# Key selection in a two-block kernel: the third query tile's rounds beside the first and second tile's, instead of behind them

## The reference

```
# i_q (512, 8 heads, 64), i_k (512, 64) layer-normed, i_w (512, 8)
rel   = relu(einsum('bqhd,bsd->bqhs', iq_b, ik))      # per block of 128 queries
score = einsum('bqh,bqhs->bqs', iw_b, rel)
score = where(key <= query, score, -inf)
_, idx = top_k(score, 128)                            # min(256, 512 // 4) = 128
```

## Time and profile before

| | us |
|---|---|
| median of three runs | 2519.91 |
| the profiled execution | 2520.09 |
| span of its trace | 2518.3 |
| TensorE busy | 2481.8 |
| VectorE busy | 1619.7 |
| ScalarE busy | 1205.7 |

### The profile page before, as it was taken

One profiled execution on the slowest core, in us unless ns is written; L12 is line 12 of the kernel. 1 busy time (PEld: TensorE's weight loads), 2 busy tenths in 40 slices (PEclk: granted clock), 3 DMA queues, 4 the chain that ended last, 5 costly groups with the idle time before them and its releaser, 6 DMA issues.

```text
span 2518.3 us, 37877 instructions
## 1 busy us (share of the span) xinstructions
PE 2481.8 (99%) x15440; PEld 2070.1 (82%) x15440; DVE 1619.7 (64%) x2585; ACT 1205.7 (48%) x2030; POOL 75.2 (3%) x114
## 2 busy tenths in 40 slices
PE   9999999999999999999999999999999999999998
PEld 7999888888877777878999888777776788888887
DVE  6888348866764554357887257766877655677733
ACT  6556244666555455245555246544333454444421
POOL 0111000000000000000110000000000000000000
PEclk9999999999999999999999999999999999999999
DMA  5776332222222222333775323211111112333232
GB/s 173 175 179 154 108 100 92 77 76 75 84 68 68 76 66 77 91 92 101 176 177 151 98 93 101 76 41 37 44 43 52 59 55 88 94 99 101 88 100 72
DMA packets 80525, 237.82 MB, mean 94 GB/s; under 512 B 8928, under 2 KB 10976, under 8 KB 80352
## 3 DMA queue, kind: packets, MB, share of 16 engines
q1 hardware_dynamic: 68832, 213.56, 27.0%
q0 software_dynamic: 10080, 18.35, 4.8%
q10 hardware_dynamic: 1440, 3.49, 0.4%
HBM read 233.27 MB, written 2.10 MB: 93 GB/s over the span
## 4 chain that ended last, share of the span: by engine, by line
PE 92%; DVE 5%; DMA 2%; ACT 1%; issue 1%; SPq 0%; ACTq 0%; DVEq 0%
PE bank L2208 22%; PE bank L2210 21%; PE bank L2209 21%; PE bank L2222 4%; PE bank L2224 4%; PE bank L2223 4%; PE bank L2441 2%; PE bank L2366 1%; PE bank L2280 1%; PE bank L2374 1%; DMA raw<-in_w2u 1%; PE bank L2360 1%; PE bank L2537 1%; PE bank L2347 1%; PE bank L2258 1%
## 5 line engine op out<-in xcount | busy, mean ns | idle before, releaser
L2208 PE MATMUL bank<-uR,hl 128*128 128x512 f32 x1684 | 685.4, 407 | 5.3 <-DVE uR L2954 2.8
L2943 DVE TENSOR_TENSOR hl<-raw,hl 128x1024 fp32r<-128x1024 f32 (+2 forms) x325 | 386.0, 1191 | 453.9 <-ACT hl L2586 452.8
L2210 PE MATMUL bank<-uR,hl 128*128 128x512 f32 x1684 | 658.3, 391 | 0.0
L2209 PE MATMUL bank<-uR,hl 128*128 128x512 f32 x1684 | 657.7, 391 | 0.0
L2586 ACT CAST hl<-raw 128x1024 fp32r<-128x1024 f32 (+2 forms) x325 | 329.8, 1020 | 207.2 <-PE bank L2210 196.1
L2208 PEld LDWEIGHTS bank<-uR,hl 128*128 128x128 f32 x1684 | 316.8, 188 | 94.8 <-issue 24.8
L2209 PEld LDWEIGHTS bank<-uR,hl 128*128 128x128 f32 x1684 | 317.1, 188 | 67.6 <-issue 7.2
L2210 PEld LDWEIGHTS bank<-uR,hl 128*128 128x128 f32 x1684 | 316.5, 188 | 67.7
L2937 DVE TENSOR_TENSOR hl<-raw,hl 128x1024 fp32r<-128x1024 f32 (+1 forms) x142 | 150.8, 1076 | 32.4 <-ACT hl L2582 29.4
L2222 PE MATMUL bank<-sum,hl 128*128 128x256 f32 x560 | 159.3, 284 | 2.5 <-DVE fA L3082 2.5
L2223 PE MATMUL bank<-sum,hl 128*128 128x256 f32 x560 | 158.7, 283 | 0.0
(11 more groups left out here) (499 smaller groups left out, 4385.5 us busy)
## 6 DMA issues: line engine op xcount, KB each, us to landing
raw<-in_win SPq DMA_DIRECT2D x147, 512.0 KB, 3.5
raw<-in_w SPq DMA_DIRECT2D x44, 512.0 KB, 3.5
raw<-in_w1u SPq DMA_DIRECT2D x54, 256.0 KB, 3.0
raw<-in_w2u SPq DMA_DIRECT2D x51, 256.0 KB, 3.1
raw<-in_w1g SPq DMA_DIRECT2D x22, 512.0 KB, 4.5
raw<-in_w2g SPq DMA_DIRECT2D x22, 512.0 KB, 4.3
raw<-in_w1d SPq DMA_DIRECT2D x16, 512.0 KB, 3.6
raw<-in_wssd SPq DMA_DIRECT2D x16, 512.0 KB, 3.5
```

The source lines that it names most:

```text
L2208: e.matmul(s.bank[:, :], h[:, 0, w], hi, start=s.first and q == 0, stop=False)
L2209: e.matmul(s.bank[:, :], h[:, 0, w], lo, start=False, stop=False)
L2210: i = e.matmul(s.bank[:, :], h[:, 1, w], hi, start=False, stop=s.last and q == n - 1)
L2943: e.tensor_tensor(h[:, 1, w], x[:, w], h[:, 0, w].bitcast(F), ALU.subtract).then_inc(*sig("dve_split.lo", s, i))
```

## The change

The third tile's indexer now stands beside a chain of the first and the second tile's, and it stands first in `both`. The signals that free the index pages now name the last score step of all three tiles, as tile 3's is no longer the last one planned.

```
-        yield from both(indexer(1), indexer(2))
-        yield from indexer(3)
-        ikp[0].release(masks[3, "x"])
+        yield from both(indexer(3), chain(indexer(1), indexer(2)))
+        done = [masks[i, "x"] for i in (1, 2, 3)]
+        ikp[0].release(*done)
         for x in iq:
-            x.release(masks[3, "x"])
+            x.release(*done)
```

## The result

| | before | after |
|---|---|---|
| median | 2519.94 us (6 runs) | 2528.49 us (6 runs, 2527.98 to 2534.56) |
| ratio to before, 95% interval | | 1.0041 [1.0031, 1.0051] |
| the profiled execution | 2520.09 us | 2528.44 us |
| span of its trace | 2518.3 us | 2526.6 us |

The change made the kernel slower: by 8.5 us, 0.34%, by the medians, and by 0.41% by the ratio over all runs. The forecast was 3.4 us faster, and the range ended at 2524.5 us. The page's first line, the answer to the earlier trace rows: the same number of matmuls, in a longer span. Of the 8.3 us that the span grew, TensorE is busy for 2.6 (2484.4 against 2481.8, which fits the same matmuls with more of them at the slow clock) and idle for 5.7.

The account below looks back on a forecast made before the run. The prediction took TensorE's waiting and slow clock as all the change could move. Terms -2.0 - 2.0 - 1.4 + 1.3 + 0.7 = -3.4 us gave 2516.7 us (2516.5 by the median), range 2510 to 2524.5 us.

Parts of the forecast that it names:

- What bounds the kernel: Whole span: TensorE is busy 2481.8 of 2518.3 us; the change can move only its waiting and slow clock.
- R4: Rival, held nearly certain and included in every case: tiles go in order 3, 1, 2 instead of two abreast.
- (a): Fourth pair's preparation: ten lighter rounds of tile 1 replace tile 2's ahead of operations TensorE awaits; 2.0 us gained.
- (b): Fourth pair's preparation: one more free page lets a panel in to fill TensorE's waits; 2.0 us gained.
- (c): Fourth pair's scan: lighter rounds stand before two TensorE waits; 1.4 us gained, bounds 0 and 2.9 us, 4.0 with clock.
- R1: Rival, chance 0.23: panel comes in whole, lighter scan rounds keep TensorE fed, both slow-clock stretches go; 2511 us.
- (d): Second and third pairs' preparation: heavier rounds, six for nine, similar VectorE work but longer single waits; 1.3 us lost.
- R3: Rival, chance 0.15: tile 3's ungated 4.4 us mask falls into the fourth pair's preparation; +5.1 us, 2525 us.
- (e): End of selection: some tile 2 rounds and its mask may be left before the sparse attention; 0.7 us lost.
- The rule that was weighed: VectorE's queue: alternating two tiles' rounds gives 0 by the skill page, up to 5.4 us by the rows; counted 0.

Follow-up runs that it names:

- experiment 6: Changed kernel with the four panels of keys and values (41 to 44) let in at four free pages in place of six: 2520.56 us, 1.0005.
- experiment 7: Kernel before the change with the four panels of keys and values let in at four free pages in place of six: 2517.63 us, 0.9991.
- experiment 12: Kernel before the change with panels 41 to 44 and also 33 and 34 let in at four free pages: 2517.85 us, 0.9997.
- experiment 1: Changed kernel with the arguments of `both` exchanged, so the chain of tiles 1 and 2 is asked first: 2522.19 us, 1.0010.
- experiment 4: Kernel before the change with every search of tile 1 done twice and the planner told its cost: 2524.72 us, 1.0019.
- experiment 10: Changed kernel with a chain of tiles 1, 3, 2 in place of `both`: 2525.12 us, 1.0025.
- experiment 5: Changed kernel, same instruction order, but fourteen of tile 3's rounds search only 256 of 512 columns, planner not told: 2525.54 us, 1.0021.
- experiment 3: Changed kernel with the mask step made to wait for the same gate as a round: 2525.65 us, 1.0023.
- experiment 8: Changed kernel with the mask step gated and the four panels of keys and values let in at four free pages: 2522.03 us, 1.0009.
- experiment 9: Changed kernel with gated mask, four panels let in at four free pages, and fourteen of tile 3's rounds searching 256 columns: 2516.82 us, 0.9991.
- experiment 2: Changed kernel with `both` taken out and tiles 3, 1, 2 written as a chain: 2533.7 us (4 runs), 1.0051.

## Why the prediction was wrong

**What bounds the kernel** held: the work did not change, and the result is TensorE's waiting and its slow clock in windows where VectorE is busy for 13.6 to 17.8 of 20 us, and in the scan for 4.8 of 5. So did **R4**: the tiles go 3, 1, 2.

**(a) and (b), -4.0 us: right in mechanism and size.** The fourth pair's preparation lost 5.29 - 1.60 = 3.7 us of waits, and the stretch at 0.50 went with them. A panel came in. Only about six rounds of tile 1 lie there, not ten. As the next term shows, (b) was not a gain.

**(c), -1.4 us, is the step that failed, and by the most: it came out at +4.4 us of waits (7.3 against 2.9), with more time at half clock.** I priced the rounds in front of two waits and took the number of waits as given, with 0 as the bound on the loss side, "since no operation gets longer". The number of waits goes with how many chunks of the scan are left when the panels stop. The panel of (b) was one of those; with it spent, TensorE had no panel for 14.1 us, nearly three chunks of 5.06 us, where before it was 5.6 us, about one. The bound was false: a wait needs no longer operation, only missing cover. The prediction asked of each stall that goes what is late next, and for (b) named only the panel's split. Experiments 6, 7 and 12 show it, from both sides. By the same reason R1, which let (b) and (c) gain together, could not come.

The moved panel is not the whole of it. In experiments 1, 4 and 10 no panel moved (208 of the L2208 matmuls ahead of the long stretch, as before, and again 256 when the panels stop), and still the scan went without panels for 8.6, 10.4 and 9.1 us and had 5.1, 5.9 and 5.5 us of waits. So where the selection's rounds and pages stand counts as well, and how much of the +4.4 us is the panel's and how much theirs was not separated.

**(d), +1.3 us: right in sign, about a third of what came.** Ten rounds of tile 3 lie there (the MATCH_REPLACE8 of 128x512 from 1700.33 to 1728.73), not six: its waits rose by 3.9 us there (6.1 against 2.2), and a further 0.56 at 1676. The selection's work there was thus not "about the same", as the count of six for nine had it, but 10 x 1.52 = 15.2 us in place of 9 x 0.98 = 8.8. Experiment 5 shows the effect, in the same order with lighter rounds. (The count of six did come true in experiment 4; why this plan let ten in was not traced.)

**R3's mechanism came true in another place.** The ungated mask did fall into a preparation, the third pair's, since ten rounds in the second had used up tile 3 early. I had asked only whether fewer than fifteen places lie before the fourth pair's preparation, and not what happens if there are more. It cost 3.5 us of waiting, which R3 put at 3, and some time at a lower clock (0.91 over 20 us). Experiment 3 shows it.

**(e), +0.7 us: about nothing.** Tile 2's last round starts at 1983.5 and its mask is done before the sparse attention needs it; the window 2000 to 2020 is full, as in the earlier trace rows. But experiments 8 and 9 have a new wait of 2.2 us at the sparse attention, on its softmax and not on a mask. That the panels used in the scan are missing beside it would be the same conservation once more, but no run tests it, and experiment 6, with the same page edit, has no such wait.

Summed by waits, (a) and (b) -3.7, (d) +4.5, the mask +3.0, (c) +4.4: +8.2 us against the 8.5 measured. The slower clock (2.6 us of busy time) and the start of this stretch, 2.5 us earlier in the trace of after (below), are not in this sum and offset each other by chance. The experiments' gains (2.8, 3.0 and 7.9 us by the medians) add up to 13.7 and give 11.7 together, or 10.8 if each time is taken against its own kernel before; they are not independent.

**The rule that was weighed** (alternating rounds) stays untested: in every run here one tile's rounds ended before the next one's began.

**Left open.** Why experiment 2 is no better, and by its medians 5 us worse, than the change though the tiles go the same way: its rounds and scores stand at other places, and I did not single one out. And whether both holes can be filled at once. In the trace of experiment 6 both are filled: the fourth pair's preparation has 1.6 us of waits, none over 0.32, and its scan has none. But its median is 3 us above that of experiment 7, since (i) and (ii) remain; in 8 and 9, where they were taken up too, the sparse attention waits longer. A form that keeps all of the gain was not found.

## What to carry to other kernels

Filler work that covers stalls is a budget: before counting a stall as gone because something moved into it, find where that something stood, and count what it covered there. Here moving panels within the budget gained nothing (experiment 12), while loosening the page rule that sets it did (experiment 6). Where a priority order lets a low-priority producer finish early, look at its ungated last step, which lands wherever it has got to. And price a fill-in operation by its single length, not only by the sum that a gate admits: the one behind it on the chain waits for the whole of it.

## What the runs showed that I had not expected

**How the clock follows the waits.** In the second pair's preparation TensorE waited 6.1 us in nine pieces over 26 us, and the granted clock was 1.00 in 1700 to 1720 and 0.91 in the 20 us behind. In experiments 3 and 8 the same nine waits, to a hundredth of a microsecond, left it at 1.00 in both windows: the waits alone do not fix the clock, and one trace is one draw. In the scan, with five waits of 0.98 to 2.38 us in 12.5 us, it fell to half. Windows of 5 us there:

```profile
1950.00:1955.00 5.00, 2.03 (x16) 0.94 (x14) 4.79 (x12) 1.58 (x2) 0.00 (x0) 0.81 0.01 3
1955.00:1960.00 5.00, 2.74 (x16) 1.39 (x16) 4.76 (x14) 0.00 (x0) 0.00 (x0) 0.50 0.00 0
1960.00:1965.00 5.00, 2.92 (x14) 1.72 (x15) 4.76 (x15) 0.00 (x0) 0.00 (x0) 0.50 0.00 0
```

Two whole windows stand at exactly 0.50, 1.2 GHz, and the panel matmuls of 1965 step by 0.43 us where those of 1949 stepped by 0.23. The Trainium skill, "TensorE: Matmul & The Clock Gate", section "What's actually happening", says that the gate knows only the half and the full rate. The trace agrees: the clock is 1.00 from 1950.0 to 1953.1 and 0.50 from 1953.3 to 1966.7, and 0.81 is a mean over both.

**The part ahead of the change moves too.** The order of TensorE's instructions is the same in both kernels up to the first score matmul near 1636. Yet the first L2399 matmul starts at 1587.7 us before, 1585.2 after, and 1590.2 in experiment 6. So up to 5 us between two profiled spans here can have nothing to do with the edit; the waits behind it are the safer measure of one trace.
